# One ScalarE copy for both heads' turned probabilities, in place of two, in the attentions of a two-block transformer kernel

## The reference, cut to what matters

```
# first block: attention A (latent, 8 heads, 96 wide) and B (grouped, 8 heads, 64 wide)
s = jnp.einsum("bqhgd,bkhd->bhgqk", qblk, k).astype(jnp.float32)
pr = jax.nn.softmax(s, axis=-1).astype(v.dtype)
return jnp.einsum("bhgqk,bkhd->bqhgd", pr, v)

# second block: forgetting attention, 16 heads, 64 wide, causal: block blk of 128 queries sees keys up to e
s = jnp.einsum("bhqd,bhkd->bhqk", q[:, :, s0:e], k[:, :, :e]).astype(jnp.float32) * scale
s = s + log_f_cum[:, :, s0:e, None] - log_f_cum[:, :, None, :e]
p = jax.nn.softmax(jnp.where(mask, s, -jnp.inf), axis=-1)
outs.append(jnp.einsum("bhqk,bhkd->bhqd", p.astype(v.dtype), v[:, :, :e]))
```

## Time and profile before

| | |
|---|---|
| median of three runs | 2181.24 us (2179.29 to 2182.57) |
| the profiled execution's own time | 2178.25 us |
| its span, first to last instruction | 2176.4 us |
| TensorE busy | 2128.5 us, 98% |
| VectorE busy | 1147.3 us, 53% |
| ScalarE busy | 814.4 us, 37% |
| granted TensorE clock, mean | 0.992 |
| `attn` in the span | from about 186 to 299 us |
| `fox` in the span | from about 1665 to 1743 us |

### The profile page before, as it was taken

The page is one execution under the profiler, slowest core; times in us unless marked ns, Lnnn a source line. Parts: engine busy times, 40 slices in busy tenths (PEclk is TensorE's granted clock), DMA queues, the critical chain, the costliest instruction groups (busy, mean ns, idle before and its releaser), DMA issues.

```text
span 2176.4 us, 26174 instructions
## 1 busy us (share of the span) xinstructions
PE 2128.5 (98%) x10774; PEld 1699.4 (78%) x10774; DVE 1147.3 (53%) x1710; ACT 814.4 (37%) x1167; POOL 36.8 (2%) x40
## 2 busy tenths in 40 slices
PE   8999999999999999999999999999999999999998
PEld 6777678888888887787977888887787777888886
DVE  5575765442542578888836444423733746444323
ACT  4324753331232364542534222212414843332212
POOL 0120000000000000000100000000000000000000
PEclk9999999999999999999999999999999999999999
DMA  4221013222222213343121222223233022222221
GB/s 173 87 78 39 2 59 107 97 93 99 80 97 97 97 64 100 114 126 96 41 97 58 97 97 97 94 84 112 67 115 129 2 97 78 93 82 97 97 97 68
DMA packets 43112, 190.69 MB, mean 88 GB/s; under 512 B 15520, under 2 KB 16224, under 8 KB 22384
## 3 DMA queue, kind: packets, MB, share of 16 engines
q1 hardware_dynamic: 40656, 184.78, 25.3%
q10 hardware_dynamic: 2336, 4.23, 0.6%
HBM read 185.25 MB, written 3.74 MB: 87 GB/s over the span
## 4 chain that ended last, share of the span: by engine, by line
PE 51%; DVE 1%; ACT 1%; issue 0%; DVEq 0%; ACTq 0%
PE psum L441 14%; PE psum L440 14%; PE psum L442 14%; PE psum L898 1%; PE psum L881 1%; PE psum L911 1%; PE psum L451 1%; PE psum L455 1%; PE psum L452 1%; PE psum L2701 0%; PE psum L2767 0%; ACT weights_high L223 0%; DVE weights_low L250 0%; PE psum L2793 0%; PE psum L2754 0%
## 5 line engine op out<-in xcount | busy, mean ns | idle before, releaser
L250 DVE TENSOR_TENSOR weights_low<-weights_raw,weights_high 128x2048 fp32r<-128x2048 f32 (+1 forms) x161 | 365.5, 2270 | 587.9 <-ACT weights_high L223 587.8
L440 PE MATMUL psum<-split,weights_high 128*128 128x512 f32 x1448 | 574.5, 397 | 6.0 <-DVE weights_low L250 3.7
L441 PE MATMUL psum<-split,weights_high 128*128 128x512 f32 x1448 | 573.4, 396 | 0.0
L442 PE MATMUL psum<-split,weights_low 128*128 128x512 f32 x1448 | 571.8, 395 | 0.0
L223 ACT CAST weights_high<-weights_raw 128x2048 fp32r<-128x2048 f32 (+1 forms) x161 | 304.0, 1888 | 572.5 <-PE psum L442 532.9
L440 PEld LDWEIGHTS psum<-split,weights_high 128*128 128x128 f32 x1448 | 271.5, 188 | 76.7 <-issue 5.2
L442 PEld LDWEIGHTS psum<-split,weights_low 128*128 128x128 f32 x1448 | 271.5, 187 | 65.3
L441 PEld LDWEIGHTS psum<-split,weights_high 128*128 128x128 f32 x1448 | 271.6, 188 | 64.5 <-issue 0.2
L441 PE MATMUL psum<-hidden_low,weights_high 128*128 128x512 f32 x256 | 102.1, 399 | 0.0
L440 PE MATMUL psum<-hidden_high,weights_high 128*128 128x512 f32 x256 | 100.9, 394 | 0.0
L442 PE MATMUL psum<-hidden_high,weights_low 128*128 128x512 f32 x256 | 100.4, 392 | 0.0
(11 more groups left out here) (484 smaller groups left out, 3073.5 us busy)
## 6 DMA issues: line engine op xcount, KB each, us to landing
weights_raw<-in_weights SPq DMA_DIRECT2D x161, 1024.0 KB, 4.9
minus_c<-minus_c_rows ACTq DMA_DIRECT2D x16, 256.0 KB, 7.5
x_stream<-in_x SPq DMA_DIRECT2D x4, 512.0 KB, 7.2
gdn_in_grown<-gdn_rows SPq DMA_DIRECT2D x4, 512.0 KB, 4.5
chain_grown<-gdn_rows SPq DMA_DIRECT2D x4, 512.0 KB, 3.5
out<-end_results SPq DMA_DIRECT2D x8, 256.0 KB, 2.1
table<-rope_tables SPq DMA_DIRECT2D x1, 1024.0 KB, 12.4
weights_raw<-in_weights SPq DMA_DIRECT2D x1, 768.0 KB, 4.2
```

What stands on the lines that cost most here:

```text
L250: self.nc.vector.tensor_tensor(out=self.low_of(n)[:, 0:width], in0=self.raw[:, n % 2, 0:width], in1=self.high_of(n)[:, 0:width].bitcast(se ...
L440: nc.tensor.matmul(bank, wh, ah, start=first, stop=False)
L441: nc.tensor.matmul(bank, wh, al, start=False, stop=False)
L442: return nc.tensor.matmul(bank, wl, ah, start=False, stop=last)
```

## The change

The two copies of a step become one instruction, which waits until both heads have been turned, reads banks 4 and 5 and writes both heads' places of `prob_t`, and raises the semaphore `turned_act` by two at its end. Nothing else is changed: TensorE and VectorE have the same instructions in the same order, and no wait on TensorE is written differently.

```
             def copies(self, act, step):
-                n = self.keys(step)
-                for u in (2 * step, 2 * step + 1):
-                    act.wait_ge(self.turned, u + 1)
-                    if step >= 3:
-                        act.wait_ge(self.attended, step - 2)
-                    nc.scalar.copy(self.prob_t[:, u % 6, 0:n], psum[:, 4 + u % 2, 0:n]).then_inc(self.turned_act, 1)
+                n, u = self.keys(step), 2 * step
+                act.wait_ge(self.turned, u + 2)
+                if step >= 3:
+                    act.wait_ge(self.attended, step - 2)
+                nc.scalar.copy(self.prob_t[:, u % 6:u % 6 + 2, 0:n], psum[:, 4:6, 0:n]).then_inc(self.turned_act, 2)
```

## The result

| | before | after |
|---|---|---|
| median of ten runs | 2180.58 us (2178.44 to 2184.51) | 2187.91 us (2183.94 to 2189.09) |
| ratio | | 1.0032, 95% interval 1.0024 to 1.0040 |
| span of the profiled execution | 2176.4 us | 2185.9 us |
| ScalarE busy | 814.4 us | 812.0 us |
| granted TensorE clock, mean | 0.992 | 0.988 |

The change is slower, by 0.24 to 0.40%. The forecast was 3.7 us more, 2185.0 in a range of 2182.3 to 2188.4; measured are 7.3 us more, 2187.91. The time lies in the range, and the movement is twice the forecast one.

What follows compares the result with a forecast made beforehand. The prediction took TensorE to set the pace, with ScalarE close behind. Stalls at five kinds of place (1.68 + 0.84 + 0.54 + 0.22 + 0.45 = 3.73 us) added to 2181.24 gave 2185.0 us, range 2182.3 to 2188.4.

Steps and rivals of the forecast that it cites:

- sign of being wrong: Forecast called wrong if attention B's cycle grows, if that of `fox` (8.39 to 8.60 us) doesn't, or if either becomes shorter.
- the rival in which ScalarE is the bound: ScalarE bounds `fox` and attention B, so its saved time counts: 2178.7 us, faster; chance 0.05.
- The rival in which a copy out of two banks is dearer: Copy from banks beside which TensorE writes takes 1.19 us: sum 6.2 us, 2187.4 us; chance 0.20.
- Place 1: `fox`, even to odd after each of eight 512-key steps: next turn 0.21 us later each, 1.68 us.
- Place 2: Start of `attn`: nothing lies between turns 0 and 1, so turn 1 comes 0.84 us later.
- Place 3: End of `attn`: turn 31 comes 0.26 us later, the last `attend` 0.54 us in sum.
- Place 4: Start of `fox`: two transposes only, turn 1 comes 0.22 us later.
- Place 5: End of `fox`: turn 30 has no scores before it and comes 0.45 us later.
- odd to even: Attention A, odd to even step: two 96-wide scores lie between, so more slack than the 0.6 us of even to odd.
- all of it is TensorE's own time: The summed 3.73 us is all TensorE time, and the projections behind start that much later.
- P's share: Follow-up theory: places where a copy stands between two TensorE turns pay; 4.3 to 4.6 us expected of the changed kernel.
- The main case: Five kinds of place stall, 3.73 us slower in sum: 2185.0 us, bounds 2183.9 to 2186.4; chance 0.60.

Runs made afterwards that it cites:

- e5: Kernel before with the single copy only in the 50 steps where slack was predicted, two copies at the other 14: 2179.72 us, ratio 0.9998.
- e0: The changed kernel once more, unaltered, beside the kernel before: 2185.63 against 2179.81 us, ratio 1.0027.
- e11: Kernel before with only turn 0 put ahead of the first scores in `attn` and `fox`: 2178.36 against 2179.53 us.
- e7: Kernel before with turn 0 ahead of the first scores in both objects and `attend` 28 ahead of turn 30 in `fox`: 2179.78 against 2181.22 us.
- e10: Kernel before with the single copy at step 0 of `attn` alone: 2180.66 us, ratio 1.0003.
- e2: Kernel before with the single copy in `fox` only, two copies in `attn`: 2183.12 us, ratio 1.0013.
- e1: Kernel before with the single copy in `attn` only, two copies in `fox`: 2182.70 us, ratio 1.0011.
- e3: Kernel before, still two copies, but the first also waits until both heads are turned: 2181.67 us, ratio 1.0010.
- e6: Changed kernel with two copies at the last two steps of `attn`: 2184.67 us, ratio 1.0016 to the kernel before.
- e8: Changed kernel with a 512-key score of `fox` moved ahead of the turn that stalls: 2185.81 us, ratio 1.0024 to the kernel before.
- e9: The kernel before, unaltered, profiled a second time: 2181.39 us, ratio 0.9999.

## Why the prediction was right or wrong

**What it said of the mechanism holds.** The cost is the path turn, copy, turn. Measured at full width it is 2.29 us at the start of `attn` and 2.33 in `fox` (forecast 2.26): 1.14 to 1.18 us from the turn to the copy (forecast 1.12), 1.01 for the copy (1.00), 0.14 from its end to the turn (0.14). It costs nothing in attention A's and B's steady parts, though B had the smallest slack, and e5 shows 50 steps at no cost. Neither sign of being wrong came: B's cycle did not grow, and that of `fox` did. The time saved on ScalarE, 4.4 us of copies, is worth nothing, as forecast: the rival in which ScalarE is the bound falls with e5 and with ScalarE's idle times. The rival in which a copy out of two banks is dearer falls with its 1013 ns.

**Place by place.** Place 1 (eight 512-key steps of `fox`): forecast 0.21 us each, measured 0.25 to 0.26 in seven, by the cycle of 8.64 to 8.65 us, and 0.19 behind the eighth (part f); in sum 1.97 us against 1.68. Place 2 (start of `attn`): 0.84, measured 0.87. Place 3 (end of `attn`): 0.54, measured 0.61 for b and c together. Place 4 (start of `fox`): 0.22, measured 0.19. Place 5 (turn 30 of `fox`): 0.45, measured 0.52 (1.90 us from turn 29 instead of 1.38). Sum 3.73, measured 4.16.

**The terms that were off.** The 0.43 us by which the copy starts later was read from the lengths of rows (1.09 less 0.66), whose ends are modelled; the starts give 0.49 (1.18 less 0.69). That is 0.05 to 0.06 us more at a full turn, and the eight 512-key steps make up 0.29 of the 0.43 us missing in the sum. And under "where it is hidden", "odd to even" was passed for all of `attn`, when turn 30 has one score before it and not two. Turn 30 is 0.24 us later by that. It adds little in the end: turn 31, for which 0.26 us had been forecast, comes 0.21 us later.

**The step that fell short** is the sentence that all of it is TensorE's own time "and the projections behind it start that much later". In it the clock has no term; it is taken as that of before. Of the 7.3 us between the medians (5.8 in e0's group), 4.2 us are the places. The rest goes with the clock. The changed kernel had a mean clock of 0.988 in 12 of its 17 runs, the kernel before in 21 of the 89 that ran beside e0 to e11. On the chip of e0 the kernel before takes 4.0 us more at 0.988 than at 0.991 (2183.27 and 2179.25 us); on the chips of the other two groups it is 2.8 and 5.3 us. The traces say the same. What they spend outside the parts a to f is 1997.9 to 1999.0 us at a mean clock of 0.992 (before, e5, e11), 1999.2 to 2000.8 at 0.990 and 0.991 (e7 to e10), 2000.4 and 2002.4 at 0.989 (e2, e1), and 2002.4 to 2005.2 at 0.988 (changed, e0, e3, e6).

The stretch behind `attn` is one such place: from L440 to the first matmul at 880 us it takes 581.04 to 581.10 us in the six traces without the low clock, and 582.6 in six of those with it (582.4 in e8), so about 1.6 us more. In e10 the end of `attn` is that of the kernel before and comes 0.45 us later, and the low clock is there. So no longer wait at the end of `attn` is needed for it. That the shift itself brought it isn't shown: the sort by position holds here and fails at 880 us, and e9 and the kernel before differ by 1.55 us with no shift to speak of. Why the changed kernel met the low clock more often than the kernel before stays open.

**What was luck.** The chances had 0.37 on slower by over 0.2% and 0.58 on within 0.2%; the first came, at 0.32%. With 4.16 us of P's share alone (0.19%) it would have been the second. And 2187.91 lies within the range only because the range reached up to the rival in which the copy is dearer, which isn't what happened. The main case had its upper bound at 2186.4.

## What to carry to other kernels

When two buffers are handed back by one instruction, the first waits for the second twice over: the copy starts when the last is full (here 1.18 us behind the turn instead of 0.69), and the first is free when the last is copied. Measure the path from use to use (here 1.4 us before, 2.3 after) and set it against the work that lies between, at each place; where the work is longer, the change costs nothing and gains nothing (50 steps of 64 here, 0.07 us in sum), and where it is shorter, the difference is paid each time (0.25 us at each of seven 512-key steps of `fox`). Look at the first and the last turns of a pipeline apart, for the work between is less there, and count it: moving work into one gap takes it out of the next (the cycle of `fox` became 8.71 to 8.79 us, from 8.64).

## What the runs showed of the hardware that was not expected

An idle stretch of TensorE of one length was followed by a granted clock of 1.00 in some traces and by a stretch at 0.50 in others. The 2.4 us at the end of `attn` have the low clock behind them in seven traces of thirteen (0.86 from 297 to 309 us, against 1.00), at a price of about 1.6 us; the 3.4 us ahead of 880 us have it in eight (0.86 or 0.93 from 876 to 900 us, against 1.00). Nor does the program settle how long such a stretch is: the kernel before, traced twice, had 0.50 for three whole microseconds in one trace and for six in the other behind one and the same wait of 2.35 us, and lost 1.55 us more by it. So a comparison of two kernels at the 0.1% level by their medians measures this as well as the change. The parts a to f, between fixed instructions, repeat within 0.02 us where nothing in them was changed, and tell the two apart.

The copies with a gap between the banks' used parts (2x384, 2x256, 2x128) lie on one line with the one without: 797, 586 and 372 ns against 1013, which is 0.83 ns an element and about 160 ns besides. The one of 2x128 is no slower than a copy of 256 out of a single bank (377 ns). So the jump from bank to bank had no price here.
